# The expert stage: turning a tile's rows ahead of its predecessor's products, and copying them ahead of the tanh and the gate

## The reference, cut to what matters

```python
hg = jnp.einsum('nd,edf->nef', hf, w_gate)      # d = 1024, f = 256, e = 16 experts
hu = jnp.einsum('nd,edf->nef', hf, w_up)
act = jax.nn.silu(hg) * hu * combine[:, :, None]
return jnp.einsum('nef,efd->nd', act, w_down).reshape(B, T, D)
```

## Time and profile before

| | |
|---|---|
| Median of three runs | 1522.22 us |
| The profiled execution: its own time | 1528.06 us |
| The profiled execution: its span, first to last instruction | 1526.3 us |
| Busy share of the span: PE, DVE, ACT, POOL | 85%, 83%, 51%, 46% |
| Expert stage: first turn to last down product | 921.7 to 1399 us |

### The profile page before, as it was taken

How to read it: one execution, slowest core, us unless ns; L and a number is a source line. 1 busy time by engine, 2 the same in 40 slices (tenths; PEclk the granted TensorE clock), 3 DMA queues, 4 the chain that set the end, 5 groups by cost and what they waited for, 6 DMA issues and landing times. The chain is left out here.

```text
span 1526.3 us, 25848 instructions
## 1 busy us (share of the span) xinstructions
PE 1302.6 (85%) x8231; PEld 721.1 (47%) x8231; DVE 1269.0 (83%) x3124; ACT 777.7 (51%) x1327; POOL 703.2 (46%) x530
## 2 busy tenths in 40 slices
PE   5488899999999999999996537999999999996665
PEld 3345455555555555555554323444444444442221
DVE  2527799999999999999998487999999999993688
ACT  2412244334444444334444206898988888884122
POOL 0112256676776766677765422222222222211786
PEclk9789999999999999999998768999999999998798
DMA  9965431111111101111111195659993554222896
GB/s 310 300 211 178 156 122 50 56 42 56 56 56 56 56 29 42 56 43 56 42 48 42 69 330 187 248 202 331 338 383 107 191 186 149 107 109 87 211 253 199
DMA packets 106688, 219.40 MB, mean 144 GB/s; under 512 B 11796, under 2 KB 71000, under 8 KB 104547
## 3 DMA queue, kind: packets, MB, share of 16 engines
q1 hardware_dynamic: 82662, 141.23, 27.3%
q0 software_dynamic: 11808, 43.00, 10.0%
q10 hardware_dynamic: 12125, 34.01, 5.7%
HBM read 166.68 MB, written 51.56 MB: 143 GB/s over the span
## 5 line engine op out<-in xcount | busy, mean ns | idle before, releaser
L1159 DVE SCALAR_TENSOR_TENSOR y_sum<-uT,w_dw_cols,y_sum 128x128 f32<-128x128 f32 (+1 forms) x1780 | 461.7, 343 | 0.0
L2107 DVE SCALAR_TENSOR_TENSOR w_gate_up_lo<-w_gate_up_ring,w_gate_up_hi 128x2048 f16<-128x2048 f16 x96 | 219.5, 2288 | 35.8 <-ACT w_gate_up_hi L2029 35.3
L2029 ACT ACTIVATE w_gate_up_hi<-w_gate_up_ring 128x2048 f16 x96 | 182.8, 1906 | 53.9 <-issue 52.8
L1401 PE MATMUL bank<-w_in_hi,hT_hi 128*128 128x512 f16 (+3 forms) x544 | 194.3, 357 | 10.6 <-ACT late L998 9.6
L2010 POOL COPY slot_index<-slot_token 128x1 int32 (+1 forms) x48 | 57.9, 1205 | 309.9 <-PE eturn L2171 305.5
L1401 PE MATMUL bank<-w_in_lo,hT_hi 128*128 128x512 f16 (+3 forms) x544 | 194.2, 357 | 0.0
L1401 PE MATMUL bank<-w_in_hi,hT_lo 128*128 128x512 f16 (+3 forms) x544 | 194.0, 357 | 0.0
L2150 PE MATMUL ps_up<-w_gate_up_hi,slot_rowsT_hi 128*128 128x512 f16 x384 | 147.2, 383 | 26.2 <-DVE slot_rowsT_lo L2132 26.0
L2150 PE MATMUL ps_up<-w_gate_up_lo,slot_rowsT_hi 128*128 128x512 f16 x384 | 146.8, 382 | 0.0
L2150 PE MATMUL ps_up<-w_gate_up_hi,slot_rowsT_lo 128*128 128x512 f16 x384 | 146.6, 382 | 0.0
L2138 DVE SCALAR_TENSOR_TENSOR w_down_lo<-w_down_ring,w_down_hi 128x2048 f16<-128x2048 f16 x48 | 109.6, 2284 | 4.1 <-ACT w_down_hi L2083 3.8
(11 more groups left out here) (302 smaller groups left out, 2873.2 us busy)
## 6 DMA issues: line engine op xcount, KB each, us to landing
expert_rows<-out_rows ACTq DMA_DIRECT2D x48, 512.0 KB, 3.1
late<-in_w_ada SPq DMA_DIRECT2D x22, 1024.0 KB, 7.3
w_gate_up_ring<-in_w_gate SPq DMA_DIRECT2D x16, 1024.0 KB, 8.7
w_gate_up_ring<-in_w_up SPq DMA_DIRECT2D x16, 1024.0 KB, 11.6
w_down_ring<-in_w_down SPq DMA_DIRECT2D x16, 1024.0 KB, 12.3
x_h<-in_x_prompt SPq DMA_DIRECT2D x16, 512.0 KB
x_res<-in_x_prompt SPq DMA_DIRECT2D x16, 512.0 KB, 3.5
hidden<-late SPq DMA_DIRECT2D x16, 512.0 KB, 2.6
```

Source lines behind the costliest of these rows:

```text
L1159: dve.scalar_tensor_tensor(total, u, w, y_sum[:, c, :n], ALU.mult, ALU.add).then_inc(taps_done, 1)
L1401: mm = pe.matmul(out, x[xp][:, k, :n], w[wp][:, k, cols], start=(k == 0 and wp == xp), stop=(k == KD - 1 and xp == 1))
L2029: act.activation(gate_up_parts[0][:, at, k:k + KD // 2, :, :].rearrange("p k a n -> p (k a n)"), w_gate_up[:, bass.ds(b, 1), k:k + KD // 2 ...
L2107: dve.scalar_tensor_tensor(flat[1], w_gate_up[:, bass.ds(b, 1), k, :, :].rearrange("p b k a n -> p (b k a n)"), W_SCALE, flat[0], ALU.mult ...
```

## The change

Three pieces of code move; nothing is added or taken away. On PE the turn of tile i goes to the start of the step, ahead of the up products of tile i-1. On ACT the two copies of tile i's rows go ahead of the tanh of tile i-1. On DVE the two `slot_rowsT_lo` go ahead of the gate and `act_tok` of tile i-1. All waits move with their instructions, and none is new.

```diff
@@ -2061,18 +2061,18 @@
                         act.dma_start(expert_rows[at, :], out_rows[:, c, :]).then_inc(stored[c], 16)
                     if turn_tile is not None:
                         split(KD // 2)
-                    if up_tile is not None:
-                        j, c = up_tile, up_tile[1] % 2
-                        act.wait_ge(up_done, count(1, j, 1))
-                        if not is_tile(j, 0):
-
-                            act.wait_ge(gate_ready, count(1, j))
-                        act.activation(gate_tanh[:], ps_up[c][:, 0, :], ACT.Tanh, scale=0.5 / W_SCALE).then_inc(tanh_ready, 1)
                     if turn_tile is not None:
                         j, c = turn_tile, turn_tile[1] % 2
                         for h in range(2):
                             act.wait_ge(turned, count(2, j, h + 1))
                             act.copy(rowsT[0][:, c, 4 * h:4 * h + 4, :], turn[h][:, :, :]).then_inc(rowsT_hi_ready, 1)
+                    if up_tile is not None:
+                        j, c = up_tile, up_tile[1] % 2
+                        act.wait_ge(up_done, count(1, j, 1))
+                        if not is_tile(j, 0):
+
+                            act.wait_ge(gate_ready, count(1, j))
+                        act.activation(gate_tanh[:], ps_up[c][:, 0, :], ACT.Tanh, scale=0.5 / W_SCALE).then_inc(tanh_ready, 1)
                     if up_tile is not None:
 
                         j, c = up_tile, up_tile[1] % 2
@@ -2114,16 +2114,6 @@
                         dve.tensor_tensor(actT[1][:], ps_act[:], actT[0][:], ALU.subtract).then_inc(actT_ready, 1)
                     if turn_tile is not None:
                         split(1)
-                    if up_tile is not None:
-                        j, c = up_tile, up_tile[1] % 2
-
-                        dve.wait_ge(tanh_ready, count(1, j, 1))
-                        dve.scalar_tensor_tensor(gate[:], gate_tanh[:], 1.0, ps_up[c][:, 0, :], ALU.add, ALU.mult).then_inc(gate_ready, 1)
-                        dve.wait_ge(gate_ready, count(1, j, 1))
-                        if not is_tile(j, 0):
-
-                            dve.wait_ge(act_turned, count(1, j))
-                        dve.scalar_tensor_tensor(act_tok[:], gate[:], 1.0 / (W_SCALE * W_SCALE), ps_up[c][:, 1, :], ALU.mult, ALU.mult).then_inc(act_ready, 1)
                     if turn_tile is not None:
                         j, c = turn_tile, turn_tile[1] % 2
                         for h in range(2):
@@ -2132,6 +2122,16 @@
                             dve.tensor_tensor(rowsT[1][:, c, k, :], turn[h][:, :, :], rowsT[0][:, c, k, :], ALU.subtract).then_inc(rowsT_ready, 1)
                     if up_tile is not None:
                         j, c = up_tile, up_tile[1] % 2
+
+                        dve.wait_ge(tanh_ready, count(1, j, 1))
+                        dve.scalar_tensor_tensor(gate[:], gate_tanh[:], 1.0, ps_up[c][:, 0, :], ALU.add, ALU.mult).then_inc(gate_ready, 1)
+                        dve.wait_ge(gate_ready, count(1, j, 1))
+                        if not is_tile(j, 0):
+
+                            dve.wait_ge(act_turned, count(1, j))
+                        dve.scalar_tensor_tensor(act_tok[:], gate[:], 1.0 / (W_SCALE * W_SCALE), ps_up[c][:, 1, :], ALU.mult, ALU.mult).then_inc(act_ready, 1)
+                    if up_tile is not None:
+                        j, c = up_tile, up_tile[1] % 2
                         b = dve.value_load(K["tile_buffer"][0:1, tile_at(j)], min_val=0, max_val=WEIGHT_RING - 1)
                         dve.wait_ge(down_hi_ready, count(1, j, 1))
                         flat = [w[:, c, :, :].rearrange("p k n -> p (k n)") for w in down_parts]
@@ -2152,6 +2152,16 @@
 
                 def step(i):
                     turn_tile, up_tile, down_tile, store_tile = stages(i)
+                    if turn_tile is not None:
+                        j, c = turn_tile, turn_tile[1] % 2
+                        pe.wait_ge(gathered[c], half(j) * 16 + 16)
+                        for h in range(2):
+                            if not is_tile(j, 0):
+
+                                pe.wait_ge(rowsT_ready, count(2, j, h - 1))
+                            for k in range(4):
+                                mm = pe.transpose(turn[h][:, k, :], rows[:, c, 4 * h + k:D:KD], ident[:])
+                            mm.then_inc(turned, 1)
                     if up_tile is not None:
                         j, c = up_tile, up_tile[1] % 2
                         pe.wait_ge(rowsT_ready, count(2, j, 2))
@@ -2160,16 +2170,6 @@
                             pe.wait_ge(act_ready, count(1, j, -1))
                         product(ps_up[c][:].rearrange("p a n -> p (a n)"), lambda k, xp, wp:
                                 (rowsT[xp][:, c, k, :], gate_up_parts[wp][:, c, k, :, :].rearrange("p a n -> p (a n)")), KD).then_inc(up_done, 1)
-                    if turn_tile is not None:
-                        j, c = turn_tile, turn_tile[1] % 2
-                        pe.wait_ge(gathered[c], half(j) * 16 + 16)
-                        for h in range(2):
-                            if not is_tile(j, 0):
-
-                                pe.wait_ge(rowsT_ready, count(2, j, h - 1))
-                            for k in range(4):
-                                mm = pe.transpose(turn[h][:, k, :], rows[:, c, 4 * h + k:D:KD], ident[:])
-                            mm.then_inc(turned, 1)
                     if down_tile is not None:
                         j, c = down_tile, down_tile[1] % 2
                         pe.wait_ge(actT_ready, count(1, j, 1))
```

More of the change, by code:

```diff
@@ L2063, in step @@
                         split(KD // 2)
+                    if turn_tile is not None:
+                        j, c = turn_tile, turn_tile[1] % 2
+                        for h in range(2):
+                            act.wait_ge(turned, count(2, j, h + 1))
+                            act.copy(rowsT[0][:, c, 4 * h:4 * h + 4, :], turn[h][:, :, :]).then_inc(rowsT_hi_ready, 1)
                     if up_tile is not None:
@@ L2070, in step @@
                         act.activation(gate_tanh[:], ps_up[c][:, 0, :], ACT.Tanh, scale=0.5 / W_SCALE).then_inc(tanh_ready, 1)
-                    if turn_tile is not None:
-                        j, c = turn_tile, turn_tile[1] % 2
-                        for h in range(2):
-                            act.wait_ge(turned, count(2, j, h + 1))
-                            act.copy(rowsT[0][:, c, 4 * h:4 * h + 4, :], turn[h][:, :, :]).then_inc(rowsT_hi_ready, 1)
                     if up_tile is not None:
@@ L2116, in step @@
                         split(1)
+                    if turn_tile is not None:
+                        j, c = turn_tile, turn_tile[1] % 2
+                        for h in range(2):
+                            dve.wait_ge(rowsT_hi_ready, count(2, j, h + 1))
+                            k = slice(4 * h, 4 * h + 4)
+                            dve.tensor_tensor(rowsT[1][:, c, k, :], turn[h][:, :, :], rowsT[0][:, c, k, :], ALU.subtract).then_inc(rowsT_ready, 1)
                     if up_tile is not None:
@@ L2126, in step @@
                         dve.scalar_tensor_tensor(act_tok[:], gate[:], 1.0 / (W_SCALE * W_SCALE), ps_up[c][:, 1, :], ALU.mult, ALU.mult).then_inc(act_ready, 1)
-                    if turn_tile is not None:
-                        j, c = turn_tile, turn_tile[1] % 2
-                        for h in range(2):
-                            dve.wait_ge(rowsT_hi_ready, count(2, j, h + 1))
-                            k = slice(4 * h, 4 * h + 4)
-                            dve.tensor_tensor(rowsT[1][:, c, k, :], turn[h][:, :, :], rowsT[0][:, c, k, :], ALU.subtract).then_inc(rowsT_ready, 1)
                     if up_tile is not None:
@@ L2154, in step @@
                     turn_tile, up_tile, down_tile, store_tile = stages(i)
-                    if up_tile is not None:
-                        j, c = up_tile, up_tile[1] % 2
-                        pe.wait_ge(rowsT_ready, count(2, j, 2))
-                        pe.wait_ge(gate_up_ready, count(2, j, 2))
-                        if reused(j):
-                            pe.wait_ge(act_ready, count(1, j, -1))
-                        product(ps_up[c][:].rearrange("p a n -> p (a n)"), lambda k, xp, wp:
-                                (rowsT[xp][:, c, k, :], gate_up_parts[wp][:, c, k, :, :].rearrange("p a n -> p (a n)")), KD).then_inc(up_done, 1)
                     if turn_tile is not None:
@@ L2172, in step @@
                             mm.then_inc(turned, 1)
+                    if up_tile is not None:
+                        j, c = up_tile, up_tile[1] % 2
+                        pe.wait_ge(rowsT_ready, count(2, j, 2))
+                        pe.wait_ge(gate_up_ready, count(2, j, 2))
+                        if reused(j):
+                            pe.wait_ge(act_ready, count(1, j, -1))
```

(2 more changed lines are left out.)

## The result

The changed kernel takes 1540.64 us (median of four runs, 1536.45 to 1548.46), beside 1522.5 us of the kernel before on the same chip. The ratio is 1.0122, with a 95% interval from 1.0080 to 1.0163: slower by 18 us, where 6.9 were forecast, and above the range. The profiled execution took 1543.2 us, its span 1541.5.

What follows compares the result with a forecast made beforehand. The prediction took a ring of waits between engines, not one engine, as the bound: 0.27 us more a pair, 5.9 over 44 tiles, plus 1.0 at the entry, on 1522.22 gives 1529.1 us; likeliest case 1523.7 to 1532.1, 8-in-10 range 1516 to 1535.

Steps and rivals of the forecast that it cites:

- The ring: Waits between PE, ACT and DVE in the expert stage, going round once in two tiles: 19.42 us before the change.
- The new one: The ring after the change, from tanh round to tanh, forecast at 19.69 us for two tiles.
- terms of 5.90, 2.05, 2.20, 1.20, 0.45 and 5.38 us: ACT's run to second weight half; DVE's low half; next DVE operation; rows' low parts; gate to `act_tok`; up products to tanh.
- `act_tok` until the up products: On PE, the turn of `act_tok` and eight row transposes before the up products: 1.79 us, bounds 1.59 and 1.88.
- the tanh until `w_down_hi`: On ACT, from tanh to `w_down_hi` with a register load between: 0.72 us, 0.34 of it idle.
- The entry: In the first step PE turns tile 1 before multiplying tile 0: about 1.0 us later, between 0 and 2.0.
- DVE's register load: Between `act_tok` and `w_down_lo` on DVE: no longer under the rows' low parts, 0.38 us more a tile, hidden by slack.
- The tanh does not wait in every step: Forecast sign: ACT's tanh would wait for the up products in every step, not in every second.
- The register load does not hide: Rival: ACT's load hides while it waits for the up products; ring 19.24 us, kernel 1519.2 us; chance 0.15.
- The waits before the up products: Rival: PE's waits for the rows' low parts simply go, regaining 20 us: 1502 us; chance 0.10.
- Transposes do overlap behind a wait: Rival said they do not: ten take 2.74 us on PE, ring 21.12, about 1560 us; chance 0.05.
- "Nothing to measure": Rival: transposes at the lower bound, 2.5 us more in all, 1524.7 us; chance 0.14.

Runs made afterwards that it cites:

- e3: The changed kernel with five unused products put into PE's wait for `act_tok`, behind the down products of odd steps: 1537.78 us, ratio 1.0093.
- e11: The changed kernel with five unused products behind PE's wait for `act_tok`, between row transposes and up products, every second step: 1574.16 us, ratio 1.0334.
- e4: The changed kernel with ACT's register load for `w_down_hi`, and the wait belonging to it, moved ahead of the copies: 1522.48 us, ratio 0.9994.
- e6: e5 with the register loads of ACT and DVE moved ahead of the copies and the rows' low parts: 1501.77 us, ratio 0.9863.
- e7: The changed kernel with DVE's part undone and the register loads of ACT and DVE moved ahead: 1502.28 us, ratio 0.9871.
- e1: The kernel before with only PE's turn of the rows moved, ACT and DVE in their old order: 1523.47 us, ratio 1.0002.
- e5: The changed kernel with PE's row transposes put ahead of the turn of `act_tok` instead of behind it: 1515.43 us, ratio 0.9949.
- e8: The kernel before with the register loads of ACT and DVE moved ahead and nothing else: 1517.59 us, ratio 0.9959.

## Why the prediction was wrong

The direction and the place were right, the size was not: +18 us, where +6.9 stood.

**What bounds the kernel.** The ring was read rightly, but for two of its terms. The new one runs through the stations that the prediction lists, once in two tiles. Its terms of 5.90, 2.05, 2.20, 1.20, 0.45 and 5.38 us were measured as 5.89, 2.05, 2.21, 1.20, 0.44 and 5.38.

**The step that failed first: `act_tok` until the up products, and the tanh until `w_down_hi`.** These are the two mis-sized terms. The first was put at 1.79 us with an upper bound of 1.88, and measured 2.02. The bound added 0.51, the duration of two that had waited, and 0.89 from eight that had not the earlier trace rows; behind the wait the two take 0.55 from start to start (with 0.24 us of idle time for "issue" in the weight loads), and the eight let the next product in after 0.99. The second was taken as 0.72 from the last tile of before; in the loop it is 0.80 (1305.20 and 1306.00). In the changed kernel's last tile, which is done outside the loop, it is 0.72 again (1407.41 and 1408.13), so that the row was right and the tile not like the others; why the loop's is 0.08 longer no run shows:

```profile
1408.13 1.91 ACT L2083 ACTIVATE w_down_hi<-w_down_ring 128x2048 f16 x1 [0.34 <-issue]
```

Together they make 0.31 us a pair (20.00 instead of 19.69), which would be 6.8 us over 22 pairs. The ring's cost measured 10.7 us, not 5.9 + 6.8 = 12.7: the last pair takes 18.8 us instead of 20.0, and in the profile before three pairs take 19.75 to 20.03 instead of 19.42.

**The step that was missing: what PE's new idle time does to its clock.** The prediction said that PE would idle ahead of the turn of `act_tok`, and put no price on it. It cost 10.3 us in the profiled run, half of the stage's loss: rows of before gave no sign of it, since there PE waits 0.37 and 0.77 us at these places. That the falls hang on this wait is shown (e3 ends them by filling it, e11 keeps both); whether the wait does it alone or with the transposes behind it, and why one in three to five is followed by a fall and the others are not, is open. The Trainium skill ("TensorE: Matmul & The Clock Gate", Part 1, HAM oscillation) describes a kernel whose clock falls again and again because TensorE waits for data between its groups of products. The runs agree with it in kind, not in number: there the clock falls at every such wait, here at six, four and eight of 22.

**The entry** was put at 1.0 us, the delay of the first up products. They start 1.2 us later against the stage's first high half of the weights (9.03 us behind it, before 7.80). At the tanh of tile 0 only 0.2 us of this is left (16.34 and 16.12), since the clock rises earlier among these products, as the lower bound had it: nine of them take about 0.6 us instead of 0.38, before fourteen. The 0.7 us up to the tanh of tile 3 are mostly the steps from tile 0 on; that the sum's 1.0 lies near it is partly luck.

**The waits.** PE waits before the turn of `act_tok`, as said, and no more before the up products; DVE's wait for the second weight half stays, 24.1 us over 44 tiles, 0.55 a tile (0.5 was said). DVE's register load came into the open as said (0.34 us) and is covered: in the same pair DVE still waits 1.07 us for ACT. The tanh does not wait in every step, as I had said, but in every second, 23 times in 44 tiles: with ACT's copies out of its way, the other step is paced by ACT itself.

**The rivals.** The register load does not hide on the ring: 0.41 us of "issue" behind each tanh that waited (1306.00), and moved ahead it gives back 0.5 us a pair (e4). Behind the tanh of 1294.66, which waits for nothing, it does hide, so that it shows in every second step and not in nearly every one, as I had said. Had it been hidden, the kernel would be at 1522.5 us, with the falls gone too (e4). The waits before the up products did not simply go; that they can go, to 1502 us, is shown by e6 and e7, but only with DVE's order or PE's place for `act_tok` put right, and the loads too. Transposes do overlap behind a wait: eight took 1.16 us, and the ring 20.0, not 21.1. "Nothing to measure" is what TensorE's part alone gives (e1). And the chances put the whole forecast down as slower, though its own range began at 1523.7, under the 1525.3 that was set for slower.

**Where the 18 us are.** 10.7 in the ring, 6.9 to 10.3 in falls of the clock (four and six of them), 0.7 at the entry: 18.3 to 21.7 by the profiles. The part behind the last tanh varies from 133 to 141 us in profiles of kernels whose code is the same there, which was not followed up; single profiles can't be set against the median more closely than that.

## What to carry to other kernels

An instruction that is issued earlier on an in-order engine stands behind other waits: here eight transposes whose rows lay ready waited for `act_tok`, and the gate for two subtractions that nothing needed yet. Ask of each moved instruction which wait it now stands behind and which ring this lengthens; in this kernel work off the ring belongs ahead of a wait, as the transposes in e5 and the register loads in e8. And where a change makes TensorE wait regularly, put a price on its clock too, and test it by filling the wait with idle work.

## What the runs showed of the hardware

- A regular wait of 1.5 us, with ten transposes behind it, in a stretch where PE is otherwise full was followed by a fall of the granted clock in six of 22 pairs, four of 22 when repeated, and eight of 22 at 1.62 us. In the changed kernel each fall made four to eight up products take 0.63 us instead of 0.38, and cost 1.72 us. Five products that are of no use, put into the wait, ended the falls and made 44 tiles 9.7 us shorter (6.3 beside the repeat).
- ACT's register load directly behind a tanh that waited shows as 0.41 us of idle time in the loop and 0.34 in the last tile, and behind the tanh of 1294.66, which waited for nothing, not at all; yet in e5 0.41 shows behind the tanh of 1299.40, for which no wait is listed. DVE's directly behind `act_tok` shows as 0.34. Read ahead of the copies, ACT's is hidden (0.28 us from the tanh to `w_down_hi` in e6).
- The eight row transposes take 1.05 us, but 1.16 to 1.29 in the rows above directly behind the two transposes of `act_tok` that waited.
- One product of two float32 128x128 operands shows as two rows, and five cost 1.11 us on the path.
